# An attention stage ahead of an MLP: new slots for its steps, a new place for the rotary tables' load and for the spread of the softmax sums

## The chip, the cores and the metric

The kernel runs on one core of a Trainium2 chip. The metric is the device time of one execution in microseconds (us); lower is better. Engines are named as in the profile: PE (TensorE, matmul; PEld its weight loads), DVE (VectorE), ACT (ScalarE), POOL (GpSimd) and SP (SyncE, which here only issues DMA transfers). Each engine works off its own list of instructions in order; they meet through semaphores.

## What is computed

One layer of a hybrid encoder on 2048 tokens of width 1024, in float32:

```python
h = rms_norm(x, norm_mix_g)
qa, ka, va, qi, ki, wi, qb, kb, vb, zb, bb, ab = split(h @ w_in)
qa, ka, qi, ki = rope(...)                      # rotary: x1*cos - x2*sin, x2*cos + x1*sin
o_a = sparse_indexer_attention(...)             # 8 heads, 2 kv heads, width 64
      # index scores choose 256 keys per query; softmax attention over these,
      # keys admitted up to the end of the query's chunk of 64
o_b = gated_deltanet(...)                       # 4 heads, width 128, chunkwise delta rule
x = x + concat(o_a, o_b) @ w_out
h = rms_norm(x, norm_ffn_g)
x = x + square(relu(h @ w_ff1)) @ w_ff2         # 1024 -> 4096 -> 1024
out = rms_norm(x, norm_final_g)
```

The kernel computes the sparse attention as dense attention over all admitted keys with a bias that is hugely negative where a key was not chosen.

## The kernel before

Three stages follow one another: norm and input projection, the DeltaNet with index scores and the first part of the selection, and `attention_and_mlp`, which begins at 1526 us and runs to the end. The change lies in the third alone.

**Units.** Attention is cut into 16 tiles of 128 queries; a tile has four units of two heads, u = 4t + q, 64 in all. The steps of a unit are: `scores` on PE (q high and q low against the keys, in pieces of 512 keys; lines 2102 and 2103), `mask` on DVE (adds the bias, keeps the maximum; 1937, 1944), `exp` on ACT (1834), `rinv` on DVE (reciprocal of the sums; 1964), then in turns of two blocks of 128 keys (one turn in tiles 0 and 1, two in tiles 2 and 3) `transpose` on PE (2117), `high` on ACT (1823), `lower` on DVE (1957) and `product` on PE (2131, first with the high half of the probabilities, then with the low half). `spread` on PE (2139) copies the reciprocals along the 64 rows of the output by a matmul with the identity; `low` on ACT (1829) fetches the second half of the product, `finish` on DVE (1920 adds, 1923 multiplies by the spread) and `store` on SP (1651) end the unit. The product accumulates in one PSUM bank, O_BANK, columns 0 to 255. Transposes, values and the spread share a ring of two banks; whoever takes a ring bank waits until the one two places before has been read.

**Preparation.** Per tile there are three items, item 3t (keys) and 3t+1, 3t+2 (queries of the two kv groups): `prep_in` on SP (six transfers, lines 479 to 481), `cos` on DVE (1970), `sin` and `add` on POOL (1710, 1717), `round` on ACT (1846) and `prep_low` (1979 on DVE for keys, 1723 on POOL for queries), which raises `p_done`. The cosine and sine tables of a tile (`table_in`, line 1608) are in one buffer. `values` (2108) transposes the tile's values, `values_hi` and `values_low` split them, `values_out` (1617) stores them to memory and `values_back` (1626) loads them for each turn. Scores of units 4t and 4t+1 wait for items 3t and 3t+1, those of 4t+2 and 4t+3 for item 3t+2 also.

**MLP.** Tokens go through it in four blocks of 512. Each of its 288 weight units is loaded (`weights`, 1594), copied to a high half by ACT (`split`, 1807), its low half made by POOL (1695), and used by three matmuls a piece (2037 to 2039). The mixed rows come by `mix_in` (1668) in two buffers, with a copy on ACT (1800) and a subtraction on DVE (1912); `mix_in(0,4)` waits for all stores of units 0 to 15. While the MLP runs, ACT also searches the selection threshold of the late tiles (`probe`, 1750).

**The order.** `OverlapPlan` puts every step of every engine in a numbered slot; within a slot the steps of an engine follow `ORDER`. A slot has no duration and no barrier: it only fixes each engine's order. Units 0 to 15 (tiles 0 to 3) stand in the slots below 0, three slots apart (`begins(u)` = 3u - 58), the first dense matmul in slot 0; later units lie among the 147 slots of an MLP block, about 8.4 apart. The first slot is -71 before, -72 after. Where the steps of a unit stand is set by `attention`, the weights and splits by `mlp`, the ring by `number`.

Slots before of the start, as the plan gives them: SP -71 weights 0 and 1, values_in 0, prep_in 0 to 4, table_in 0; POOL -70 split 0 and 1, sin 0, add 0; -64 sin 1, add 1; PE -61 scores 0. SP at the end: -14 prep_in 14; -11 prep_in 15, table_in 5; -9 store 15, mix_in 0.

## Time and profile before

| | us |
|---|---|
| median of 3 runs | 3991.24 |
| lowest and highest | 3988.57 and 3998.67 |
| profiled execution, its own time | 3992.01 |
| its span (first to last instruction) | 3990.2 |
| PE busy | 3455.4 (87%) |
| ACT busy | 2182.6 (55%) |
| DVE busy | 2082.6 (52%) |
| POOL busy | 1373.3 (34%) |

The span cut into 40 equal slices of 99.8 us; a digit is the busy share in tenths, PEclk the TensorE clock granted, in tenths of full speed. The third stage begins in the 16th slice.

```profile
PE   6799847888888994578999879999888999988997
PEld 5688736777777773457777658787667878867886
DVE  5233036777777753445455465656457575433222
ACT  3212137666745543376966858696776944333232
POOL 3201043424254432223434323433323333334442
PEclk8899979999999996799999989999999999999999
```

### The profile page before, as it was taken

To read this page: it belongs to the slowest core of one execution; us is meant where nothing else is said; L and a number is where in the kernel's file an instruction comes from. 1 tells how busy PE (TensorE), PEld (TensorE's weight loads), DVE (VectorE), ACT (ScalarE), POOL (GpSimd) and SP (SyncE) were. 2 spreads that over 40 slices of the span, in tenths; PEclk is the share of its full clock that TensorE was granted. 3 is DMA by queue.
4 is the path that set the end of the run, shared out by engine and by line. 5 is a ranking of instruction groups with operands and counts; after the bars stand their busy time and mean duration, and the time that the engine had idled before them with its cause. 6 is when DMAs were issued, how large, how long until landed. Compare 5 with 4: busy or idle time off the path is not lost.

```text
span 3990.2 us, 47621 instructions
## 1 busy us (share of the span) xinstructions
PE 3455.4 (87%) x16994; PEld 2821.0 (71%) x16994; DVE 2082.6 (52%) x3582; ACT 2182.6 (55%) x3722; POOL 1373.3 (34%) x721
## 2 busy tenths in 40 slices
PE   6799847888888994578999879999888999988997
PEld 5688736777777773457777658787667878867886
DVE  5233036777777753445455465656457575433222
ACT  3212137666745543376966858696776944333232
POOL 3201043424254432223434323433323333334442
PEclk8899979999999996799999989999999999999999
DMA  3612162313332333323333333333333333342222
GB/s 106 248 63 79 64 171 60 111 50 76 100 81 79 85 124 106 101 86 96 107 109 115 97 118 105 124 106 113 111 118 108 109 101 105 100 132 80 97 97 71
DMA packets 326091, 409.63 MB, mean 103 GB/s; under 512 B 26065, under 2 KB 241233, under 8 KB 321489
## 3 DMA queue, kind: packets, MB, share of 16 engines
q1 hardware_dynamic: 320528, 370.94, 30.7%
q10 hardware_dynamic: 5328, 35.65, 2.3%
q8 instruction: 137, 2.24, 0.2%
q14 instruction: 98, 0.79, 0.1%
HBM read 331.62 MB, written 74.87 MB: 102 GB/s over the span
## 4 chain that ended last, share of the span: by engine, by line
PE 29%; ACT 16%; DVE 7%; issue 5%; POOL 2%; SPq 1%; DMA 1%; ACTq 0%; DVEq 0%; POOLq 0%
PE m_ps L2037 8%; PE m_ps L2039 8%; PE m_ps L2038 8%; ACT m_junk L1750 7%; ACT m_wh L1807 2%; PE m_ps L2131 2%; PE m_ps L2117 2%; ACT m_prob L1834 1%; ACT m_verdict L1752 1%; ACT m_trial L1756 1%; ACT m_phi L1823 1%; PE m_ps L2102 1%; PE m_ps L2080 1%; PE m_ps L2103 1%; ACT m_rl L1766 1%
## 5 line engine op out<-in xcount | busy, mean ns | idle before, releaser
L1695 POOL TENSOR_TENSOR m_wl<-m_raw,m_wh 128x1024 fp32r<-128x1024 f32 x288 | 715.2, 2484 | 1414.7 <-ACT m_wh L1807 1414.7
L2037 PE MATMUL m_ps<-m_ah,m_wh 128*128 128x512 f32 x1280 | 536.6, 419 | 71.4 <-DVE m_al L1896 42.2
L2039 PE MATMUL m_ps<-m_ah,m_wl 128*128 128x512 f32 x1280 | 512.5, 400 | 0.0
L2038 PE MATMUL m_ps<-m_al,m_wh 128*128 128x512 f32 x1280 | 511.2, 399 | 0.0
L2037 PE MATMUL m_ps<-m_th,m_wh 128*128 128x512 f32 x1024 | 428.7, 419 | 41.5 <-DVE m_tl L1876 25.1
L2039 PE MATMUL m_ps<-m_th,m_wl 128*128 128x512 f32 x1024 | 407.5, 398 | 0.0
L2038 PE MATMUL m_ps<-m_tl,m_wh 128*128 128x512 f32 x1024 | 406.3, 397 | 0.0
L1750 ACT ACTIVATE m_junk<-m_sc,m_trial 128x1152 int8<-128x1152 f32 (+7 forms) x248 | 401.6, 1619 | 1.3
L1807 ACT ACTIVATE m_wh<-m_raw 128x1024 fp32r<-128x1024 f32 x288 | 302.7, 1051 | 126.7 <-PE m_ps L2039 122.3
L2037 PEld LDWEIGHTS m_ps<-m_ah,m_wh 128*128 128x128 f32 x1280 | 247.4, 193 | 137.9 <-DVE m_al L1896 31.3
L1874 DVE TENSOR_TENSOR m_rl<-m_rl 128x512 f32<-128x512 f32 x128 | 93.8, 733 | 413.0 <-ACT m_th L1770 412.7
L1153 DVE SCALAR_TENSOR_TENSOR i_score<-i_relu,i_w,i_score 128x512 f32<-128x512 f32 (+3 forms) x266 | 272.3, 1031 | 50.3 <-ACT i_relu L1018 36.7
L1869 DVE TENSOR_TENSOR m_acc<-m_acc,m_ps 128x512 f32<-128x512 f32 x256 | 174.9, 684 | 231.6 <-PE m_ps L2039 230.0
L1823 ACT ACTIVATE m_phi<-m_ps 128x512 fp32r<-128x512 f32 (+1 forms) x288 | 163.9, 570 | 226.4 <-PE m_ps L2117 222.5
L2039 PEld LDWEIGHTS m_ps<-m_ah,m_wl 128*128 128x128 f32 x1280 | 247.2, 193 | 55.3
L2038 PEld LDWEIGHTS m_ps<-m_al,m_wh 128*128 128x128 f32 x1280 | 248.4, 194 | 47.6 <-issue 3.4
L1957 DVE TENSOR_TENSOR m_plo<-m_ps,m_phi 128x512 fp32r<-128x512 f32 (+1 forms) x288 | 189.2, 658 | 148.7 <-ACT m_phi L1823 147.3
L2037 PEld LDWEIGHTS m_ps<-m_th,m_wh 128*128 128x128 f32 x1024 | 196.7, 192 | 91.8 <-issue 34.4
L274 PE MATMUL ps<-xh,wh 128*128 128x512 f32 x576 | 226.9, 394 | 21.2 <-POOL wl L154 19.2
L1018 ACT ACTIVATE i_relu<-i_ps 128x512 f32<-128x512 f32 (+3 forms) x304 | 155.8, 544 | 148.8 <-PE i_ps L817 121.9
L2039 PEld LDWEIGHTS m_ps<-m_th,m_wl 128*128 128x128 f32 x1024 | 196.3, 192 | 43.7
L2038 PEld LDWEIGHTS m_ps<-m_tl,m_wh 128*128 128x128 f32 x1024 | 197.3, 193 | 41.6 <-issue 5.3
(306 smaller groups left out, 7559.9 us busy)
## 6 DMA issues: line engine op xcount, KB each, us to landing
m_raw<-w_units SPq DMA_DIRECT2D x288, 512.0 KB, 3.6
m_vals<-valsT SPq DMA_DIRECT2D x256, 128.0 KB, 3.7
p_raw<-w_proj SPq DMA_DIRECT2D x72, 256.0 KB, 3.9
projT<-work ACTq DMA_DIRECT2D x12, 1024.0 KB, 3.9
g_qkvz<-projT SPq DMA_DIRECT2D x16, 768.0 KB, 6.2
wraw<-w_proj SPq DMA_DIRECT2D x21, 512.0 KB, 3.5
projT<-p_out SPq DMA_DIRECT2D x36, 256.0 KB, 3.0
work<-xT SPq DMA_DIRECT2D x8, 1024.0 KB, 5.5
```

The lines of the kernel that those rows point to most:

```text
L274: nc.tensor.matmul(acc, wh[:, u, kc, :], xh[:, kc, tok], start=(kc == 0), stop=False)
L1018: nc.scalar.activation(relu[:, c % RELUS, 0:w], ips[:, c % 2, 0:w], ACT.Relu).then_inc(relu_done, 1)
L1153: nc.vector.scalar_tensor_tensor(out=to, in0=relu[:, c % RELUS, 0:w], scalar=w_idx[:, j, h:h + 1], in1=to, op0=ALU.mult, op1=ALU.add).then ...
L1695: nc.gpsimd.tensor_tensor(wl[:, n % 3, :], raw[:, n % 2, :], wh[:, n % 3, :].bitcast(fp32), ALU.subtract).then_inc(w_lo, 1)
L1750: turns.do(nc.scalar.activation(junk[:, 0:N], sc[:, 0:N], ACT.Sign, scale=-1.0, bias=trial[:, :].bitcast(fp32), accum_out=balance[:, :]))
L1807: nc.scalar.activation(wh[:, n % 3, :], raw[:, n % 2, :], ACT.Copy).then_inc(w_hi, 1)
L1823: nc.scalar.activation(p_hi[:, m % 2, 0:w], t_bank(r)[:, 0:w], ACT.Copy).then_inc(hi_done, 1)
L1869: nc.vector.tensor_tensor(acc[:, k, :], acc[:, k, :], f_bank(c), ALU.add).then_inc(y_added, 1)
L1957: nc.vector.tensor_tensor(p_lo[:, m % 2, 0:w], t_bank(r)[:, 0:w], p_hi[:, m % 2, 0:w].bitcast(fp32), ALU.subtract).then_inc(lo_done, 1)
L2037: nc.tensor.matmul(dst, hi, rh, start=first, stop=False)
L2038: nc.tensor.matmul(dst, hi, r_low, start=False, stop=False)
L2039: return nc.tensor.matmul(dst, lo, rh, start=False, stop=last)
```

## The change

It has four parts. (1) The first tables are loaded ahead of the rotated rows, and weights 0 to 3 after them; `table_in(t)` waits for the sine and cosine of the last item that uses the tables instead of for its low half. (2) The steps of a preparation item stand one slot or more apart, the first query item of a tile a unit sooner. (3) For units 0 to 15 (`alone`) mask, exp, high, lower, low, finish, store and the values' steps each move a slot or two later. (4) The spread goes to columns 256 to 511 of O_BANK and is put ahead of the first product of its unit, for all 64 units; it waits for `finish` of the unit before, and leaves the ring.

```diff
-        "sp": "weights store values_in values_out values_back prep_in table_in ...
+        "sp": "weights store values_in values_out values_back table_in prep_in ...
-        "pe": "product spread scores values transpose dense squares".split(),
+        "pe": "spread product scores values transpose dense squares".split(),
...
-        self.first = self.begins(-4) - 1
+        self.first = self.begins(-4) - 2
...
-            a = self.begins(4 * t + {"k": -4, 0: -2, 1: -1}[what])
-            prep_slot[i], prep_done[i] = a, a + 1
             before = i - 5 if i < 12 else 9 if i == 12 else i - 1
-            self.put("sp", self.first if before < 0 else prep_done[before] + 1, "prep_in", i, before)
+            load = self.first + (i > 0) if before < 0 else prep_done[before] + 1
+            a = max(self.begins(4 * t + {"k": -4, 0: -3, 1: -1}[what]), load + 2)
+            prep_at[i], prep_done[i] = a, a + 3
+            self.put("sp", load, "prep_in", i, before)
             self.put("dve", a, "cos", i)
-            for k in ("sin", "add"):
-                self.put("pool", a, k, i)
-            self.put("act", a + 1, "round", i)
-            self.put("dve" if what == "k" else "pool", a + 1, "prep_low", i)
+            self.put("pool", a, "sin", i)
+            self.put("pool", a + 1, "add", i)
+            self.put("act", a + 2, "round", i)
+            self.put("dve" if what == "k" else "pool", a + 3, "prep_low", i)
...
-            self.put("sp", self.first if t < 1 else prep_done[3 * t - 1] + 1, "table_in", t)
-            self.put("sp", self.first if t < 1 else self.begins(4 * t - 6) + 1, "values_in", t)
+            self.put("sp", self.first if t < 1 else prep_at[3 * t - 1] + 1, "table_in", t)
+            self.put("sp", self.first + 1 if t < 1 else self.begins(4 * t - 6) + 1, "values_in", t)
             a = self.begins(4 * t - 2)
-            kept[t] = a + 1
-            self.put("sp", a + 1, "values_out", t)
+            alone = 4 * t - 2 < 16
+            kept[t] = a + 1 + 2 * alone
+            self.put("sp", kept[t], "values_out", t)
             self.put("pe", a, "values", t)
-            self.put("act", a, "values_hi", t)
-            self.put("dve", a, "values_low", t)
+            self.put("act", a + alone, "values_hi", t)
+            self.put("dve", a + 2 * alone, "values_low", t)
...
+            alone = u < 16
...
                 self.put("pe", s, "scores", u, h, p)
-                self.put("dve", s, "mask", u, h, p)
-                mask_slot[u, h, p] = s
+                mask_slot[u, h, p] = s + alone
+                self.put("dve", s + alone, "mask", u, h, p)
                 if p == self.pieces(t) - 1:
-                    self.put("act", s + 1, "exp", u, h)
+                    self.put("act", s + 1 + alone, "exp", u, h)
...
                 self.put("pe", c + gap * i, "transpose", u, i)
-                self.put("act", c + gap * i, "high", u, i)
-                self.put("dve", c + gap * i, "lower", u, i)
-                end = c + gap * i + 2
+                self.put("act", c + gap * i + alone, "high", u, i)
+                self.put("dve", c + gap * i + 2 * alone, "lower", u, i)
+                end = c + gap * i + 2 + alone
+                if i == 0:
+                    self.put("pe", end, "spread", u)
                 self.put("pe", end, "product", u, i)
...
-            self.put("pe", end, "spread", u)
-            self.put("act", end, "low", u)
-            self.put("dve", end, "finish", u)
-            self.put("sp", end + 1, "store", u)
+            self.put("act", end + alone, "low", u)
+            self.put("dve", end + 2 * alone, "finish", u)
+            self.put("sp", end + 1 + 2 * alone, "store", u)
...
-            self.put("sp", self.first if n < 2 else self.first + 2 if n < 4 else self.unit_slot[n - 4] + 1, "weights", n)
-            s = self.unit_slot[n - 2] if n >= 2 else self.first + 1
+            self.put("sp", self.first + 2 if n < 2 else self.first + 3 if n < 4 else self.unit_slot[n - 4] + 1, "weights", n)
+            s = self.unit_slot[n - 2] if n >= 2 else self.first + 5
...
-        self.ring = [x for x in pe if x[0] in ("transpose", "spread", "values")]
+        self.ring = [x for x in pe if x[0] in ("transpose", "values")]
...
+        spread_bank = ps[0:HD, O_BANK, 2 * P:4 * P]
...
             def table_load(t):
                 if t:
-                    sp.wait_ge(p_done, 3 * t)
+                    sp.wait_ge(p_sin, 3 * t)
+                    sp.wait_ge(p_cos, 3 * t)
...
             def finish(u):
...
-                dve.wait_ge(ring_done, r + 1)
-                nc.vector.tensor_tensor(o, o, t_bank(r)[0:HD, 0:2 * P], ALU.mult).then_inc(norm_done, 1)
+                nc.vector.tensor_tensor(o, o, spread_bank, ALU.mult).then_inc(norm_done, 1)
...
             def invert(u):
                 dve.wait_ge(exp_done, 2 * u + 2)
                 if u >= 2:
-                    dve.wait_ge(ring_done, plan.ring_at["spread", u - 2] + 1)
+                    dve.wait_ge(pv_done, plan.turn[u - 2, 0] + 1)
...
             def product(u, i):
...
-                if i == 0 and u:
-                    pe.wait_ge(sum_done, u)
...
             def spread(u):
-                bank = ring_bank(plan.ring_at["spread", u])
+                if u:
+                    pe.wait_ge(norm_done, u)
                 pe.wait_ge(rinv_done, u + 1)
                 for h in range(2):
-                    last = nc.tensor.matmul(bank[0:HD, h * P:(h + 1) * P], rinv[:, u % 2, h:h + 1].to_broadcast([P, HD]),
-                                            ident[:, :], start=True, stop=True)
-                last.then_inc(ring_done, 1)
+                    nc.tensor.matmul(spread_bank[:, h * P:(h + 1) * P], rinv[:, u % 2, h:h + 1].to_broadcast([P, HD]),
+                                     ident[:, :], start=True, stop=True)
```

## Rows read from the trace of the kernel before

**Rows 1.** Stretches: from:to us, length, busy us (instructions) per engine, clock, DMA share, GB/s.
```profile
core 0: us, PE busy (x) PEld busy (x) DVE busy (x) ACT busy (x) POOL busy (x), PEclk, DMA share, GB/s
1526.00:1696.00 170.00, 76.80 (x308) 55.84 (x308) 66.27 (x207) 53.66 (x135) 52.17 (x49) 0.63 0.39 111
1526.00:1583.00 57.00, 12.79 (x42) 8.77 (x42) 12.23 (x45) 12.17 (x32) 19.85 (x22) 0.50 0.45 132
...
1850.00:3400.00 1550.00, 1434.14 (x6903) 1165.11 (x6902) 916.06 (x1644) 1107.73 (x1793) 555.59 (x264) 0.96 0.36 110
```

**Rows 2.** Timeline of the start: start us, us, engine line, what [idle before <- releaser].
```profile
1527.27 0.91 SPq L1594 DMA_DIRECT2D m_raw<-w_units  x2
...
1528.69 0.58 SPq L479 DMA_DIRECT2D m_acc<-projT  x1
...
1530.85 1.06 ACT L1807 ACTIVATE m_wh<-m_raw 128x1024 fp32r<-128x1024 f32 x1 [3.33 <-DMA m_raw<-w_units]
...
1531.98 4.64 POOL L1695 TENSOR_TENSOR m_wl<-m_raw,m_wh 128x1024 fp32r<-128x1024 f32 x2 [5.43 <-ACT m_wh L1807]
...
1546.08 0.43 SPq L1608 DMA_DIRECT2D m_table<-cosT  x1
1546.55 0.43 SPq L1608 DMA_DIRECT2D m_table<-sinT  x1
...
1548.68 0.42 DVE L1970 TENSOR_TENSOR m_acc<-m_acc,m_table 128x256 f32<-128x256 f32 x1 [26.16 <-DMA m_table<-sinT]
...
1555.06 1.26 POOL L1723 TENSOR_TENSOR m_qlo<-m_acc,m_qhi 128x512 fp32r<-128x512 f32 x1 [0.74 <-ACT m_qhi L1846]
...
1556.37 0.48 PE L2102 MATMUL m_ps<-m_keys,m_qhi 128*128 128x128 f32 x1 [23.06 <-POOL m_qlo L1723]
```

**Rows 3.** Timeline of tiles 0 and 1: table issue, product(1,0), scores(4).
```profile
1566.91 0.43 SPq L1608 DMA_DIRECT2D m_table<-cosT  x1
...
1573.37 0.58 PE L2131 MATMUL m_ps<-m_phi,m_vals 128*128 128x256 f32 x1 [8.58 <-DVE m_att L1920]
...
1583.39 0.58 PE L2102 MATMUL m_ps<-m_keys,m_qhi 128*128 128x256 f32 x1 [2.44 <-POOL m_qlo L1723]
```

**Rows 4.** Waits of PE, 1596 to 1675 us: us in total, times, longest.
```profile
PE m_ps L2102 <- POOL m_qlo L1723: 6.8, 3, 3.0
PE m_ps L2131 <- DVE m_att L1920: 4.8, 1, 4.8
PE m_ps L2131 <- DMA m_vals<-valsT: 3.8, 1, 3.8
```

**Rows 5.** Timeline: scores of units 5 and 6, and a product of unit 15.
```profile
1587.57 0.58 PE L2102 MATMUL m_ps<-m_keys,m_qhi 128*128 128x256 f32 x1
...
1593.09 0.58 PE L2102 MATMUL m_ps<-m_keys,m_qhi 128*128 128x256 f32 x1
...
1673.60 0.79 PE L2131 MATMUL m_ps<-m_plo,m_vals 128*128 128x256 f32 x2 [2.51 <-DVE m_plo L1957]
```

**Rows 6.** Timeline of the tail: last scores wait, mix loads, PE's restart.
```profile
1666.77 0.50 PE L2102 MATMUL m_ps<-m_keys,m_qhi 128*128 128x512 f32 x1 [1.73 <-POOL m_qlo L1723]
...
1683.81 15.97 SPq L1668 DMA_DIRECT2D m_tmp<-mixT  x8
...
1695.21 1.09 PE L2117 MATMUL m_ps<-m_ident,m_prob 128*128 128x128 f32 x4 [15.88 <-ACT m_prob L1834]
```

**Rows 7.** Waits of ACT, 1700 to 3990 us: us in total, times, longest.
```profile
ACT m_qhi L1846 <- POOL m_rot L1717: 38.8, 12, 8.7
...
ACT m_keys L1846 <- POOL m_rot L1717: 14.9, 7, 4.5
```

**Rows 8.** Chain that ended last: start us, us, what (first and last of 17).
```profile
1816.58 1.30 POOL m_rot L1717
...
2814.57 1.30 POOL m_rot L1717
```

**Rows 9.** Lines 2139 and 1923: xcount, ns min/median/max, first and last start us.
```profile
L2139 PE MATMUL m_ps<-m_ident,m_rinv x256: 272/273/477, 1562.2 to 3487.1; 128*64 128x128 f32 x128
...
L1923 DVE TENSOR_TENSOR m_att<-m_att,m_ps x64: 411/412/415, 1573.3 to 3487.8; 64x256 f32<-64x256 f32 x64
```

More of the change, by code:

```diff
@@ L1312 @@
     ORDER = {
-        "sp": "weights store values_in values_out values_back prep_in table_in bias_in score_in x_in mix_in out bias_out".split(),
+        "sp": "weights store values_in values_out values_back table_in prep_in bias_in score_in x_in mix_in out bias_out".split(),
         "pool": "split bias_set sin add prep_low".split(),
@@ L1375, in attention @@
     def attention(self):
-        prep_done, prep_slot, mask_slot, kept, product_slot = {}, {}, {}, {}, []
+        prep_at, prep_done, mask_slot, kept, product_slot = {}, {}, {}, {}, []
         for i, (t, what) in enumerate(self.prep_items):
-            a = self.begins(4 * t + {"k": -4, 0: -2, 1: -1}[what])
-            prep_slot[i], prep_done[i] = a, a + 1
             before = i - 5 if i < 12 else 9 if i == 12 else i - 1
-            self.put("sp", self.first if before < 0 else prep_done[before] + 1, "prep_in", i, before)
+            load = self.first + (i > 0) if before < 0 else prep_done[before] + 1
+            a = max(self.begins(4 * t + {"k": -4, 0: -3, 1: -1}[what]), load + 2)
+            prep_at[i], prep_done[i] = a, a + 3
+            self.put("sp", load, "prep_in", i, before)
@@ L1915, in finish @@
             def finish(u):
-                o, r = att[:, u % 2].rearrange("p a b -> p (a b)"), plan.ring_at["spread", u]
+                o = att[:, u % 2].rearrange("p a b -> p (a b)")
                 if u >= 2:
@@ L2087, in ring_bank @@
                         pe.wait_ge(lo_done, plan.turn[tuple(x)] + 1)
-                    elif what == "spread":
-                        pe.wait_ge(norm_done, x[0] + 1)
                     else:
```

## The prediction

> **What bounds the kernel now.** I read the stretches first, then the waits of the first attention units in order of time, then the waits of the MLP part. In the stretches [rows 1] the reader is to see that from 1526 us (third stage starts) to 1696 us (first output-projection matmul) TensorE is busy for 77 of 170 us at a mean granted clock of 0.63 (0.50, that is 1.2 GHz, for the first 57 us), while from 1850 to 3400 us it is busy for over 90% at 0.96. No engine is full in these 170 us: DVE adds up to 66, ACT to 54, POOL to 52. So the chain of steps is what counts there, and it has four parts.
> The head: SP issues two weights, the values and five rotated loads before the two tables. A rotated load is six transfers, and five loads take 17.4 us of issue (1528.69 to 1546.08), 3.47 each. So the tables go out at 1546.08 and 1546.55, the first multiply by cosine starts at 1548.68 and the first scores at 1556.37 [rows 2].
> Tile 1: its table is issued at 1566.91 behind rotated loads; the multiply, add and round of its keys stand behind it, and on ACT low(0) behind that round, and product(1,0) on PE waits 8.58 us [rows 3]. scores(4) starts at 1583.39 after waiting 2.44 us for POOL's low half of the queries.
> Tiles 2 to 4: PE waits 6.8 us in three waits for low halves of queries, 4.8 for DVE's finish (itself behind a table), 3.8 for a values transfer [rows 4] and 2.51 for a lower that stands behind a cosine [rows 5]: 17.9 us together. A unit that meets no such wait takes about 5.5 us (scores at 1587.57 and 1593.09) [rows 5].
> The tail: item 13 is done when PE's scores start at 1666.77, but SP then has two rotated loads (14, and 15 behind the end of 14), a table, values and a store to issue before the first mix load at 1683.81. The mix loads go in pairs, each with a copy and a subtraction, and PE starts again at 1695.21 after 15.88 us of idle [rows 6].
> In the MLP part PE's clock is 0.96 and its waits are short. ACT idles 38.8 us before 12 roundings of queries and 14.9 us before 7 of keys, all for POOL's add [rows 7]; 17 pieces of POOL and DVE on the rotated rows stand in the chain that ended last between 1816 and 2816 us, 21.9 us together; the group shows the first and the last [rows 8].
>
> **The change, part by part.** The profiled execution took 3992.01 us (span 3990.2, 1.8 around it); the median of the three runs is 3991.24, 0.8 less. The sum is made against 3992.
>
> Head. SP now issues tables (0.95), rotated load 0 (3.47), values, rotated loads 1 to 4 (13.9), and then weights. From 1527.27 the tables go out until 1528.2, load 0 until 1531.7; 2.1 us later (the sine table of tile 0 took 2.13 from issue to multiply [rows 2]) the first sine and cosine start, at 1533.8 instead of 1548.7. That is 15 us ahead, and I let none of it reach the scores: POOL's slot of item 1 holds split(0) and split(1) ahead of its sine. Weights are now issued at 1546.1 and 1546.6 behind 24 transfers; ACT's split came 3.58 us after the issue [rows 2], so 1549.7; its two copies take 1.06 each, POOL's first subtraction starts at 1550.8 and two take 4.64, to 1555.4. Then sine (1.26), add (1.26), round and the low half with its 0.74 before it (2.0): 1560.0. First scores 3.7 us later than now: +3.7.
>
> Tile 1. SP: weights 2 and 3 wait for the two splits (1555.4), rotated load 5 follows, load 6 waits for item 1 (1560.0) and is issued until 1563.4, values_out(0) lands 2 us later, four values_back (1.74), then the table, out by 1568.6 and landed at 1570.3: 0.8 later than now. Two steps now stand behind it: cos(3) precedes mask(1) and lower(0) on DVE, sin(3) precedes prep_low(2) on POOL, so scores(2) comes at 1572.5 instead of 1563.2. But items 4 and 5 are then off the path: cosine before mask, add and round a slot apart, and the 2.44 us wait of scores(4) goes. Two units of 5.3 us follow: scores(4) at 1583, as now. Head and tile 1 together: 0 (bounds -8, if the splits' transfers land before load 1 is used up, to +6, if load 7, which waits for prep_low(2), delays item 7).
>
> Tiles 1 to 4. Of the 17.9 us of waits [rows 4, 5]: the low-half waits (6.8) go, since sine, add, round, low have slots of their own and the cosine stands ahead of the masks; the 2.51 goes, cos(14) now stands behind lower(15,1); the values wait (3.79) stays in half, the eight x loads being issued next to it as before. The table's 4.80 becomes about 2: table(2) waits for sine and cosine of item 5, not for its low half, and by the queue's order I have it out at 1588, some 5 us ahead of now. That takes away 14. Against it: the spread needs its bank back, so PE waits for finish's second step, 0.41 us more than for its first, and mask(u+1) now comes ahead of finish(u-1) on DVE. The spread's four passes (0.27 us each at the full clock, 0.48 at the most [rows 9]) only move ahead of the product. Twelve units by 0.41 are 4.9; I charge 6. Sum -8. Following the slots gives the same: 1583 + 4 units of 5.5 + 2 for the table is scores(8) at 1607; eight units of 5.8 + 0.5 and 2 for the values make scores(16) 1659, for 1666.8 now [rows 6]. Bounds: -17.9 (nothing comes in place) and +7 (every wait stays and each unit pays 0.41 and a collision).
> The row shows 0.41 us for the step that reads the spread [rows 9]. The Trainium skill (PSUM — Partial Sum Buffer, Terms and rules) says that TensorE's writes and VectorE's reads of one bank and quadrant must be kept apart by semaphores whatever the columns. By it the spread's new place beside the product makes the next product wait for the normalisation as well; over all 64 units that would be 26 us if nothing hid it, and in the MLP part, where units are 30 us apart, the trace has nothing that waits so long. It bears out the charge and is no other result.
>
> Tail. mix_in(0,0) stands behind table_in(5), which now waits for sine and cosine of item 14 and no longer for its low half; rotated load 15 moves behind mix_in(0,2), store(15) too. From p_done of item 13 the way to the first mix load is 3.47 (load 14) + 2.4 (landing, estimated from the table's 2.13) + 1.3 (sine) + 0.95 (tables) + 0.9 (values) = 9 us, now 17 (1666.8 to 1683.8) [rows 6]. That is -8; load 15 between the third and fourth mix load gives 3.5 back. Sum -4.5 (bounds -11 to +3.5).
>
> MLP part. Items of later tiles get a slot (about 3.5 us) between cosine, add, round and low: ACT's 53.7 us of idle before the rounding mostly go, but PE only gains what was on its path. From below that is 0, from above 21.9 [rows 8]; I take -5, near the lower end, since probes, weight copies and relus queue on ACT anyway and take the place. The bound above zero: queries of the first half are now rounded a unit sooner and may have to wait for scores(4t-3); if each of 12 did so for as long as the mean of today's wait for POOL (3.2 us [rows 7]) and a fifth of it reached the end, that is +8.
>
> Sum: 0 - 8 - 4.5 - 5 = -17.5 on 3992: 3975.
>
> **The rivals.**
> A, slower: the table becomes the gate of each tile. prep_low(3t+2) on POOL stands behind sin(3t+3), mask(4t+1) and lower behind cos(3t+3), and the table is issued behind values_out, its 2 us landing and values_back. If at tiles 2, 3 and 4 this costs 8.6 us as at tile 1 (now about 6 in all), 20 us are added, the 8 of those tiles go and the head's 3.7 is not won back: 20 + 3.7 - 4.5 - 5 = +14, 4006. It decides as soon as the table lands over 5 us behind the last mask of the tile before. For it: SP carries some 17 us of issue per tile against 25 to 30 us. Against: now the table costs less with each tile (8.6, then 4.8 [rows 3, 4], then no wait of PE named by it) with SP as full.
> B, nothing moves: the waits on prep are replaced by PE's wait for finish, tail and MLP give only 4: 3988. For it: DVE and PE have the most work in the stretch (66 and 77 us [rows 1]) and pass it to each other twice a unit. Against: the largest of PE's waits there has POOL as its releaser, not DVE [rows 4].
> C, more: waits for prep go whole (-14 instead of -8), the tail gives 8, ACT's freed time reaches PE (-15): 3992 - 37 = 3955. The clock helps it: the stretch runs at 0.63 [rows 1], and if fewer gaps raise it, each matmul nears 0.27 from 0.48 us [rows 9].
>
> **How the numbers follow.** Forecast 0.50, A 0.13, B 0.22, C 0.15. The forecast's own range is 3963 to 3985. Over all cases 3951 to 4001 leaves out the far half of A and the end of C. What a measurement can tell from no change is 0.3%, 12 us: below 3979 or above 4003. Faster: 0.40 of the forecast and C: 0.55. Same: the other 0.10 and B: 0.32. Slower: A, 0.13.
>
> **What would show it.** Head: first cosine near 1534, and 20 us later the first split of POOL, first scores near 1560. If scores start before 1556 the splits weren't the gate. Tile 1: scores(4) near 1583, DVE idle before cos(3) until 1570. Tiles: no wait of scores for POOL's low half, PE's waits before the spread for DVE's finish of 0.5 to 1.5 us each. Tail: first dense matmul at 1683 (a gap of some 13 us to 1696 is the first three terms). MLP: ACT's idle before the rounding under 20 us, and the time from the first dense matmul to the end 5 us under its present 2294. Wrong would be a table wait at tiles 2 to 4 above 5 us (A), or the first dense matmul past 1692 (B).

## The result and the profile after

The changed kernel takes 3951.68 us (median of 4 runs, 3948.2 to 3953.18) against 3989.9 (4 runs, 3986.85 to 3998.67) on the same chip: 0.990 of the time, 95% interval 0.9888 to 0.9912. I had forecast 3975, so 38 us went where 17.5 were announced. The profiled executions are 39.3 us apart (3992.01 and 3952.70). A few executions of the kernels below ran in a second, slower state (one of 5547.6 us, at a granted clock of 0.58 where the others have 0.94); they count in no figure here.

The first view is the two stretches that answer to [rows 1]: the third stage up to its first output-projection matmul, and the MLP part.

```profile
core 0: us, PE busy (x) PEld busy (x) DVE busy (x) ACT busy (x) POOL busy (x), PEclk, DMA share, GB/s
1522.00:1678.00 156.00, 66.33 (x308) 52.59 (x309) 67.54 (x208) 53.56 (x136) 53.49 (x49) 0.65 0.43 121
...
1850.00:3400.00 1550.00, 1440.45 (x6992) 1169.15 (x6991) 912.47 (x1660) 1116.33 (x1800) 560.25 (x262) 0.97 0.36 110
```

To compare executions I read six times from each timeline, from the stage's first instruction on (a memset on POOL): the first scores of units 0, 4, 8 and 16, the first matmul of the output projection ("dense"), and from there to the end of the span.

| kernel | unit 0 | unit 4 | unit 8 | unit 16 | dense | dense to end |
|---|---|---|---|---|---|---|
| before | 30.4 | 57.5 | 85.8 | 140.8 | 170.0 | 2294.2 |
| changed | 34.4 | 56.9 | 78.2 | 129.8 | 155.0 | 2273.4 |
| changed again | 34.6 | 57.0 | 77.7 | 130.6 | 156.6 | 2272.8 |

So 15.0 us are gained ahead of the dense matmuls, 20.9 behind them, and 3.4 more because this execution's third stage began sooner (1522.53 for 1525.94 us); over all profiled executions here, whose first two stages are the same, that start varies from 1517.5 to 1528.0. The same rows cut at these two times split the later part, the last row being the kernel before's:

```profile
1677.55:3950.90 2273.35, 2092.17 (x9823) 1689.08 (x9821) 1171.26 (x2049) 1408.36 (x2249) 828.90 (x374) 0.96 0.34 105
```
```profile
1695.95:3990.20 2294.25, 2105.44 (x9823) 1701.79 (x9821) 1179.82 (x2049) 1407.80 (x2250) 823.16 (x374) 0.96 0.34 104
```

The same 9823 matmuls take 13.3 us less, and PE's idle time falls from 188.8 to 181.2.

The start, which answers to [rows 2, 3], in a timeline (start us, us, engine, line, what, idle before and its releaser):

```profile
1523.86 0.43 SPq L1614 DMA_DIRECT2D m_table<-cosT  x1
...
1529.79 0.99 DVE L1975 TENSOR_TENSOR m_acc<-m_acc,m_table 128x256 f32<-128x256 f32 x1 [10.66 <-DMA m_acc<-projT]
...
1542.67 10.04 SPq L1599 DMA_DIRECT2D m_raw<-w_units  x4
...
1547.70 4.64 POOL L1701 TENSOR_TENSOR m_wl<-m_raw,m_wh 128x1024 fp32r<-128x1024 f32 x2 [16.05 <-ACT m_wh L1813]
...
1552.30 1.27 POOL L1716 TENSOR_TENSOR m_acc<-m_acc,m_table 128x512 f32<-128x512 f32 x1
...
1556.96 0.47 PE L2105 MATMUL m_ps<-m_keys,m_qhi 128*128 128x128 f32 x1 [26.11 <-POOL m_qlo L1729]
...
1564.28 0.36 SPq L1614 DMA_DIRECT2D m_table<-cosT  x1
```

The first cosine runs 7.3 us after the stage's start instead of 22.7. Then POOL stands idle for 16.05 us before the first weight's subtraction, which its list puts ahead of the sine of item 1. The scores come 4.0 us later than before.

PE's waits from 1522 to 1677 us, in place of [rows 4] (columns as there):

```profile
PE m_ps L2141 <- DVE m_att L1928: 29.5, 15, 6.6
PE m_ps L2105 <- POOL m_qlo L1729: 27.1, 2, 26.1
...
PE m_ps L2120 <- ACT m_prob L1840: 13.1, 1, 13.1
...
PE m_ps L2132 <- DMA m_vals<-valsT: 2.9, 1, 2.9
```

Of the waits for low halves of queries only the first of the kernel is left (26.1) and one of 1.0 us, the last item's. In their place stand fifteen waits of the spread (line 2141) for DVE's finish, 29.5 us together and 0.6 to 6.6 us each, where I had expected 0.5 to 1.5 each. The tail, against [rows 6]:

```profile
1652.35 0.79 PE L2105 MATMUL m_ps<-m_keys,m_qhi 128*128 128x512 f32 x1 [1.01 <-POOL m_qlo L1729]
...
1661.84 0.42 SPq L1674 DMA_DIRECT2D m_tmp<-mixT  x1
...
1671.80 9.78 SPq L1674 DMA_DIRECT2D m_tmp<-mixT  x5
...
1676.81 1.09 PE L2120 MATMUL m_ps<-m_ident,m_prob 128*128 128x128 f32 x4 [13.12 <-ACT m_prob L1840]
```

The first mix load leaves 9.5 us after the last tile's scores, as computed (9), where it was 17.0; three of the eight leave before rotated load 15 and five behind it, from 1671.80 on.

And ACT's waits for POOL's add from 1700 us on, 53.7 us in [rows 7]:

```profile
ACT m_qhi L1852 <- POOL m_rot L1723: 6.2, 9, 2.7
```

### The profile page after: what moved, and what is told of

Same layout as the page of the kernel before. It is cut to its first block, busy times and chain, and to the rows that moved or that the text cites. A ratio compares the mean times of both kernels' runs of the same rounds, so it can differ in the third digit from the quotient of the medians.

```text
span 3950.9 us, 47570 instructions
## 1 busy us (share of the span) xinstructions
PE 3424.2 (87%) x16994; PEld 2799.0 (71%) x16994; DVE 2075.0 (53%) x3582; ACT 2183.2 (55%) x3722; POOL 1383.3 (35%) x721
## 4 chain that ended last, share of the span: by engine, by line
PE 30%; ACT 14%; DVE 8%; issue 5%; POOL 2%; DMA 1%; SPq 1%; ACTq 0%; DVEq 0%; POOLq 0%
PE m_ps L2042 8%; PE m_ps L2044 8%; PE m_ps L2043 8%; ACT m_junk L1756 6%; ACT m_wh L1813 2%; PE m_ps L2132 2%; PE m_ps L2120 2%; ACT m_prob L1840 1%; POOL m_wl L1701 1%; ACT m_verdict L1758 1%; ACT m_trial L1762 1%; PE m_ps L2105 1%; PE m_ps L2106 1%; PE m_ps L2085 1%; ACT m_phi L1829 1%
## 5 line engine op out<-in xcount | busy, mean ns | idle before, releaser
L2042 PE MATMUL m_ps<-m_th,m_wh 128*128 128x512 f32 x1024 | 426.7, 417 | 43.1 <-DVE m_tl L1882 22.7
L1962 DVE TENSOR_TENSOR m_plo<-m_ps,m_phi 128x512 fp32r<-128x512 f32 (+1 forms) x288 | 188.8, 656 | 135.5 <-ACT m_phi L1829 134.3
L1942 DVE CUSTOM_DVE_ANT_0 m_prob<-m_ps,m_bias 128x512 f32<-128x512 f32 (+3 forms) x320 | 191.6, 604 | 87.9 <-PE m_ps L2106 83.5
```

The lines of the kernel that those rows point to most:

```text
L1942: nc.vector.tensor_tensor_reduce(out=prob[:, u % 2, h, 512 * p:512 * p + w], in0=s_bank(n)[:, 0:w], in1=bias[:, 512 * p:512 * p + w], scal ...
L1962: nc.vector.tensor_tensor(p_lo[:, m % 2, 0:w], t_bank(r)[:, 0:w], p_hi[:, m % 2, 0:w].bitcast(fp32), ALU.subtract).then_inc(lo_done, 1)
L2042: nc.tensor.matmul(dst, hi, rh, start=first, stop=False)
```

## The experiments

Each kernel is one part of the change put into the kernel before, or the changed kernel with one thing altered. Ratios are to the kernel before on the same chip, with 95% intervals. Such a ratio is good to about 0.3% when two chips are compared: the kernel with early and late preparation stands at 0.9873 on one and 0.9903 on another. The stage times are gathered in one table behind the experiments; they come from one profiled execution each, and two executions of the same kernel differ by 1.6 us (changed) and 3.1 us (tables first) in the start of the dense matmuls.

**The later preparation alone.** Items of tiles 4 and up get the new slots, their query item starts a unit sooner, and the tables of tiles 5 and up wait for sine and cosine only; all else is as before.

```diff
+            old = t < 4
+            a = max(self.begins(4 * t + {"k": -4, 0: -3, 1: -1}[what]), load + 2)
+            if old:
+                a = self.begins(4 * t + {"k": -4, 0: -2, 1: -1}[what])
...
+            self.put("pool", a if old else a + 1, "add", i)
+            self.put("act", a + (1 if old else 2), "round", i)
+            self.put("dve" if what == "k" else "pool", a + (1 if old else 3), "prep_low", i)
```

> The kernel before with one part of the change: preparation items of tiles 4 to 15 get their new slots (cosine and sine in slot a, add a+1, round a+2, low half a+3, first query item a unit sooner); all else as before. Theory 1 (the MLP part gained 18 us because ACT no longer stands before a rounding for POOL's add: 53.7 us of that idle became 6.2): ACT's wait for POOL's add from 1700 us on falls below 15 us, first dense matmul stays within 3 us of 1696, and the time is 15 to 20 us shorter, 3970 to 3975. Theory 2 (the spread's new place gave it): ACT's waits fall as well but the time stays within 5 us of before, 3985 to 3995.

3963.05, 0.9939 (0.9924 to 0.9954): -24 us, a little more than the 15 to 20 expected; 21.5 lie behind the first dense matmul. So this part alone gives what the changed kernel gains there (20.9), four times my term. In its trace the idle before the rounding is 8.2 us:

```profile
ACT m_qhi L1856 <- POOL m_rot L1727: 8.2, 10, 3.2
```

PE's idle time behind the first dense matmul is 172.3 us, 16.5 less than before, its busy time 5.1 less. The chain that ended last still has 17 pieces of POOL and DVE on the rotated rows in it, 20.4 us together (before: 17 and 21.9). So here the gain did not come out of these pieces.

**The later rounding alone.** ACT's rounding and the low half behind it move two slots later, for tiles 5 and up; cosine, sine and add stay. The later loads and tables on SP, which the plan puts behind the low half, move with it.

```diff
-            self.put("act", a + 1, "round", i)
-            self.put("dve" if what == "k" else "pool", a + 1, "prep_low", i)
+            self.put("act", a + (1 if t < 5 else 3), "round", i)
+            self.put("dve" if what == "k" else "pool", a + (1 if t < 5 else 3), "prep_low", i)
```

> The kernel before, with ACT's rounding and the low half behind it two slots later for items of tiles 5 to 15, and nothing else: cosine, sine and add stay in slot a, the first query item is not sooner. Theory 1 (the loss was ACT's: it stood before the rounding for POOL's add while its own relus and weight copies waited behind it): nearly all of late_only's 24 us, 3963 to 3970, and ACT's wait for POOL's add from 1700 us below 15 us. Rival (POOL's sine and add in one slot are the loss: POOL waits there for DVE's cosine and its weight subtraction comes late): at most a third of it, 3980 to 3988, though ACT's wait falls as well.

3970.61, 0.9944 (0.9928 to 0.996): -22. Behind the first dense matmul the gain is 16.7 us for the 21.5 of the late preparation, and the next kernel, which spaces all the steps, is 9.6 us faster on the same chip. So moving the rounding gives two thirds to three quarters of it. What it leaves is POOL's own wait for DVE's cosine, 28.7 us in this part as before, which the late preparation lowers to 7.5; whether the rest of the gain comes from that was not tested. ACT then waits once for POOL's add:

```profile
ACT m_qhi L1853 <- POOL m_rot L1724: 0.4, 1, 0.4
```

**The later preparation without the unit's lead.** As the first kernel, with -2 in place of -3.

> late_only without its other half: items of tiles 4 to 15 are spaced (sine a, add a+1, round a+2, low half a+3), but the first query item of a tile keeps its place two units ahead instead of three. Theory 1 (the spacing is what counts): within 4 us of late_only, 3961 to 3968. Rival (the unit sooner counts, since now two items of a tile stand a unit apart and share one buffer): half of the gain is lost, 3972 to 3980.

3961.0, 0.9926 (0.9911 to 0.994), 2 us under the late preparation, on another chip: the query item's earlier start isn't needed. In the trace, too, the two are close (dense matmuls 1.3 us sooner, the part behind them 4.6 us longer).

**The rounding sooner.** The wait is made larger: for tiles 5 and up the rounding stands in the add's own slot, a slot ahead of where it was.

```diff
-            self.put("act", a + 1, "round", i)
+            self.put("act", a + (1 if t < 5 else 0), "round", i)
```

> The kernel before with ACT's rounding one slot sooner for items of tiles 5 to 15, in the slot of the cosine (low half as before): ACT stands before it from the cosine's slot on. Theory (ACT's idle before the rounding reaches the end at about 0.4 us per us, 21 us for 50 us): its idle there grows from 54 us to 90 to 130 us and the time by 15 to 30 us, 4005 to 4020. Rival (only what was on the path already counts, further idle of ACT is hidden by the work queued ahead of PE): within 6 us of before.

4061.49, 1.0193 (1.0176 to 1.021): 77 us slower where I had expected 15 to 30. ACT now waits 143.9 us:

```profile
ACT m_qhi L1853 <- POOL m_rot L1724: 99.0, 22, 8.7
...
ACT m_keys L1853 <- POOL m_rot L1724: 44.9, 11, 6.6
```

That is 90 us more than before, and the part behind the first dense matmul takes 72.3 us more, 0.8 per us of ACT's idle. Taking the 53.7 us away gave 0.3 (16.7 of 53.3, the later rounding) to 0.5 (21.5 of 45.5, the later preparation). The direction of the theory held, the size missed by more than twofold. Where it reaches PE can be read from PE's waits for the high half (line 1823 of before), which ACT's list puts behind the rounding, from the first dense matmul on, first in the kernel before and then here:

```profile
PE m_ps L2131 <- ACT m_phi L1823: 6.5, 6, 1.8
```
```profile
PE m_ps L2138 <- ACT m_phi L1830: 34.1, 15, 8.0
```

**The early preparation alone.** Items of tiles 0 to 3 get the new slots, and their tables wait for sine and cosine only.

```diff
-                if t:
+                if t and t > 4:
                     sp.wait_ge(p_done, 3 * t)
+                elif t:
+                    sp.wait_ge(p_sin, 3 * t)
+                    sp.wait_ge(p_cos, 3 * t)
```

> The kernel before with one part of the change: preparation items of tiles 0 to 3 get their new slots and the tables of tiles 1 to 4 wait for sine and cosine; loads of the start, steps of the units and spread as before. Theory 1 (the waits of scores for POOL's low half and for the table are what the first 16 units lost): scores(8) some 5 us sooner, first dense matmul 8 to 12 us sooner (it also takes item 15's load out of the way of the first mix load), time 3978 to 3983. Rival (the steps of the units must move as well, else the cosine only blocks another step): first dense matmul within 3 us of 1696 and time within 4 us of before.

3973.79, 0.9962 (0.9947 to 0.9977): -15. The dense matmuls start 15.7 us sooner, where I had expected 8 to 12; half of it is there by unit 4 (-7.9), most of it by unit 8 (-13.7), and the way from unit 16 to dense is 28.1 us for 29.2. Tables leave 20.2, 36.5, 56.5 and 77.2 us after the stage's start, before 20.1, 41.0, 67.6 and 93.7. PE's waits for low halves, from the stage's start to dense, before and then here:

```profile
PE m_ps L2102 <- POOL m_qlo L1723: 32.3, 5, 23.1
```
```profile
PE m_ps L2112 <- POOL m_qlo L1733: 30.3, 4, 22.3
```

They hardly fall. What went are the two waits of a unit's first product for DVE's finish, 8.58 and 4.80 us [rows 3, 4], both of which I had put down to the tables.

**The head alone.** Tables first, one more slot of lead, weights 0 to 3 and the splits behind the rotated loads.

```diff
-            self.put("sp", self.first if n < 2 else self.first + 2 if n < 4 else ...
-            s = self.unit_slot[n - 2] if n >= 2 else self.first + 1
+            self.put("sp", self.first + 2 if n < 2 else self.first + 3 if n < 4 else ...
+            s = self.unit_slot[n - 2] if n >= 2 else self.first + 5
```

> The kernel before with one part of the change: first tables loaded ahead of the rotated rows, weights 0 to 3 after them, their splits five slots later. Theory 1 (POOL's two splits gate item 1): first cosine 15 us sooner but first scores 3 to 5 us later, and no gain at the first dense matmul: 3988 to 3996. Rival (the head start is worth something once items of tile 0 are done early): first scores before 1556 and time 5 to 15 us shorter.

3984.51, 0.9998 (0.9987 to 1.001). The first scores come at 34.7 instead of 30.4 us and the dense matmuls at 166.6 for 170.0, a difference that the timed runs don't bear out.

**The spread alone.** Its place in O_BANK, its wait for the finish before, no ring.

```diff
-        self.ring = [x for x in pe if x[0] in ("transpose", "spread", "values")]
+        self.ring = [x for x in pe if x[0] in ("transpose", "values")]
```

> The kernel before with one part of the change: the spread in columns 256 to 511 of the product's bank, ahead of the first product of its unit, waiting for finish of the unit before, and out of the ring. Theory 1: nothing to gain in the MLP part (its trace had 3 us of waits on the ring), in the first 16 units the wait for finish costs 0.4 us a unit: 3990 to 3997. Theory 2 (the spread frees the ring and PE in the MLP part): 3970 to 3980, all of it after the first dense matmul.

3985.88, 0.9996 (0.9987 to 1.0006): nothing. Behind the dense matmul PE is busy for 9.2 us less and idle for 4.8 more; the attention ahead of it takes 3.6 us longer. What it wins in the one part it gives back in the other.

**Early and late preparation together.** The two kernels above in one.

> The kernel before with the new slots for the preparation items of all tiles and nothing else (start, units and spread as before). Theory (the change's gain is the sum of its two preparation parts, 15 and 24 us, and its three other parts give nothing): 3948 to 3956, the changed kernel's own time. Rival (the parts overlap, one wait freed twice): 3960 to 3968.

3942.6 (median of three), 0.9873 (0.9852 to 0.9894): -51. The stages are read from its second measurement:

> early_late again, beside the changed kernel. Theory (only the preparation's slots gain, the rest of the change costs 0 to 6 us through the later head): 3944 to 3952, at or a little below the changed kernel. Rival (the rest is worth something too): 4 us or more above the changed kernel.

3946.24, 0.9903 (0.9889 to 0.9918): -39, the sum of 15 and 24; the first measurement was more than that. Beside it on the same chip stood the changed kernel:

> The changed kernel itself, run beside the other two so that they are compared on one chip: ratio to before 0.988 to 0.991, as when it was first measured.

3949.88, 0.9911 (0.9896 to 0.9926). The intervals overlap: the kernel with the old head and the old spread is at least as fast, and the rest of the change costs 0 to 4 us.

**Another head: tables ahead of the rotated rows, weights 0 and 1 still first.** To early and late preparation one exchange in the order of SP is added; the splits stay where they were.

```diff
-        "sp": "weights store values_in values_out values_back prep_in table_in ...
+        "sp": "weights store values_in values_out values_back table_in prep_in ...
```

> The kernel before with the new slots for preparation items of all tiles (early_only and late_only together) and one change of the start: the tables go ahead of the rotated rows in the first slot, while weights 0 and 1 stay ahead of both and their splits stay where they were. Units and spread as before. Theory (the head start is eaten in the change by the two splits, which stand ahead of item 1 and wait for weights loaded last): splits are done by 1537, first scores 14 us sooner than now at 1542, the table of tile 1 goes out some 8 us sooner, and with the 39 us of the two parts the time is 3935 to 3943. Rival (the first tiles are bound by SP's queue, so scores(4) comes when it did): 3947 to 3955.

3940.85, 0.9876 (0.9859 to 0.9892). The first scores come at 17.9 us:

```profile
PE m_ps L2107 <- POOL m_qlo L1728: 18.6, 4, 10.4
...
PE m_ps L2136 <- DMA m_vals<-valsT: 10.9, 1, 10.9
```

The second line is why little of this lasts: the first product now waits 10.9 us for its values, 3.5 in the kernel with the old head.

The second measurement shares its chip with early_late_2 and changed_again:

> table_first again, beside the changed kernel and early_late. Theory (first scores 14 us sooner and the tables of the next tiles with them): 8 to 14 us below the changed kernel and 4 to 10 below early_late. Rival (SP's queue gives the head start back): within 3 us of early_late.

3941.66, 0.9892 (0.9877 to 0.9906): 8 us under the changed kernel, 4.6 under the one with the old head. Of the 12 us by which its first scores are sooner, 4 are left at unit 4 and 2 to 5 at dense.

**The changed kernel with its splits out of the way.** Weights 0 and 1 in slot first + 13, their splits in first + 22, weights 2 and 3 in first + 25.

```diff
-            self.put("sp", self.first + 2 if n < 2 else self.first + 3 if n < 4 else ...
-            s = self.unit_slot[n - 2] if n >= 2 else self.first + 5
+            self.put("sp", self.first + 13 if n < 2 else self.first + 25 if n < 4 else ...
+            s = self.unit_slot[n - 2] if n >= 2 else self.first + 22
```

> The changed kernel with weights 0 and 1 loaded in slot first + 13, their splits in first + 22 and weights 2 and 3 in first + 25, where POOL idles in tile 1. Theory (as for table_first: POOL's splits gate the head): first scores near 1540 instead of 1557, first dense matmul 6 to 10 us sooner, time 3941 to 3946. Rival (POOL and ACT have no room in tile 1 and the splits cost there what they cost at the head): within 4 us of the changed kernel's 3952.

3939.77, 0.987 (0.9854 to 0.9886): first scores at 17.0, dense at 143.7, 12 us under the changed kernel's first measurement (another chip). What held its first scores at 34.4 us were the two splits on POOL.

**The changed kernel with the start of the kernel before, tables first.**

> The changed kernel with the start of table_first: weights 0 and 1 ahead of the tables in the first slot, their splits a slot later, weights 2 and 3 two slots later; all else as changed. If table_first's 11 us over the changed kernel come from the start alone: 3936 to 3943. If they come from the old slots of the units and the old place of the spread: 3948 to 3954.

3942.68, 0.9873 (0.9854 to 0.9891), 9 us under the changed kernel's first measurement, dense at 144.3: much the same gain by the other way, leaving the weights first in SP's queue.

**Without the later unit slots.** `alone = 0` in the changed kernel.

> The changed kernel with the steps of units 0 to 15 back in their old slots (mask, exp, high, lower, low, finish, store and the values' steps); all else as changed. Theory (these shifts change who stands behind whom, but no wait of the 16 units that counts): within 5 us of the changed kernel's 3952. Rival (they are what takes the cosine and the low half out of the units' way): first dense matmul 8 to 15 us later and time 3960 to 3967.

3947.5 (median of four), 0.989 (0.9869 to 0.9911), dense at 153.5: the slots of units 0 to 15 did not need to move.

**The handshake of the spread.** In the changed kernel the spreads of units 0 to 15 alternate between banks 0 and 1, which the MLP uses only later; a spread waits for the finish two units back, the product for the first step of the finish before it.

```diff
-        spread_bank = ps[0:HD, O_BANK, 2 * P:4 * P]
+        spread_bank = lambda u: ps[0:HD, u % 2, 0:2 * P] if u < 16 else ps[0:HD, O_BANK, 2 * P:4 * P]
```

> The changed kernel with the spread of units 0 to 15 alternating between PSUM banks 0 and 1, which are free until the first dense matmul: the spread waits for finish of two units before, and the product for finish's first step alone. It measures the handshake that the prediction charged with 6 us (PE's waits before the spread for DVE's finish are 29.5 us in all in the changed kernel). Theory (DVE is behind in any case, since finish stands behind two masks; the handshake itself is 0.4 us): waits move from the spread to the product, gain 0 to 4 us. Rival (the whole 29.5 us are the handshake's): first dense matmul 10 us sooner or more, 3942 or less.

3946.89, 0.9881 (0.9864 to 0.9898). Dense comes at 149.7 us for 155.0 and 156.6, so this handshake cost 5 to 7 us, 3 to 4 of them between units 4 and 16, for which I had charged 6; I then expected 0 to 4 in all. Single executions differ by up to 3 us here, and the medians by 3 to 5, so only its rough size is shown. PE's wait for DVE's finish, now by the product, is 12.6 us shorter:

```profile
PE m_ps L2136 <- DVE m_att L1926: 16.9, 10, 5.9
```

| kernel | unit 0 | unit 4 | unit 8 | unit 16 | dense | dense to end |
|---|---|---|---|---|---|---|
| late preparation | 30.4 | 57.3 | 85.6 | 142.6 | 166.5 | 2272.7 |
| later rounding | 30.5 | 57.6 | 86.0 | 143.3 | 172.2 | 2277.5 |
| late, without lead | 30.5 | 57.5 | 85.9 | 141.4 | 165.2 | 2277.3 |
| rounding sooner | 30.5 | 57.4 | 85.7 | 140.7 | 169.5 | 2366.5 |
| early preparation | 29.6 | 49.6 | 72.1 | 126.2 | 154.3 | 2295.9 |
| head | 34.7 | 59.1 | 83.8 | 137.6 | 166.6 | 2293.1 |
| spread | 30.6 | 58.0 | 86.7 | 145.2 | 173.6 | 2289.8 |
| early and late | 29.5 | 49.6 | 71.3 | 124.8 | 148.9 | 2272.9 |
| tables first | 17.9 | 45.2 | 67.7 | 119.8 | 143.5 | 2272.2 |
| tables first, again | 18.0 | 45.4 | 67.9 | 122.5 | 146.6 | 2275.1 |
| splits later | 17.0 | 46.4 | 68.1 | 117.7 | 143.7 | 2271.6 |
| old start, tables first | 17.9 | 48.5 | 70.2 | 118.2 | 144.3 | 2273.9 |
| unit slots as before | 34.2 | 53.9 | 76.9 | 128.2 | 153.5 | 2271.4 |
| two banks | 34.5 | 55.2 | 77.5 | 125.0 | 149.7 | 2272.6 |

The last column falls into two groups with one outlier: whatever has the late preparation is between 2271 and 2278, whatever lacks it between 2289 and 2296, and the kernel with the rounding sooner is at 2366. The changes ahead of dense leave that column alone within some 3 us. The spread alone takes 4.4 off it and the late preparation 21.5, but the changed kernel, which has both, only 20.9.

## Why the prediction was wrong

**Head, +3.7: right.** First scores 4.0 us later; the subtractions, the sine and the low half ran in the order and at the lengths that I had laid out (POOL's pair 4.64 us, then 1.27 and 1.26). Splits later and tables first show that it was the splits on POOL, as said. What I did not see is that the change left 16 to 17 us of first scores, and some 9 to 12 us of time, lying in this spot.

**Tile 1, up to scores(4) 0: right in sum.** 57.5 became 56.9.

**Tiles 1 to 4, -8: the sum close, its parts only half borne out.** From unit 4 to unit 16 the changed kernel takes 72.9 us for 83.3, so -10.4. The handshake costs 3 to 4 us of that stretch by single traces, not 6 (two banks -3.1 to -3.8, the spread alone +3.9). With it, the waits removed come to the 14 that I had named; but the early preparation without the handshake gains only 6.7 us between these units, after 7.9 ahead of them, and in it 4.9 of the 6.8 us of low-half waits that I had struck out are still there. What its trace has lost are the waits that I had put down to the tables: the table of tile 2 leaves 4.7 us sooner in the changed kernel, as I had counted (5), and 11 in the early preparation. Rival A's gate (the table) did not close at all: in the changed kernel the second table leaves at 41.8 us, 0.8 later than before as computed, but the third at 62.9 for 67.6 and the fourth at 83.1 for 93.7.

**Tail, -4.5: right.** The first mix load leaves 9.5 us after the scores for 17.0, and from unit 16 to dense it is 25.2 us for 29.2, so -4.0. The gap before the restart is 13.12 for 15.88.

**MLP part, -5: wrong, and this is the step that failed.** It measured -20.9, and -21.5 with the late preparation alone. ACT's idle before the roundings fell as forecast (under 20 us, measured 6.2); mis-sized was what that is worth. I wrote that PE gains only what was on its path, and took a value near the lower end "since probes, weight copies and relus queue on ACT anyway and take the place". The later rounding refutes that sentence: with nothing moved to an earlier slot and the roundings' wait gone, the part is 16.7 us shorter, 12.2 of it PE's idle time (188.8 to 176.6 us). Rows of before show how such a wait reaches PE, and the 8.7 of [rows 7] pointed at them:

```profile
2162.07 1.05 ACT L1807 ACTIVATE m_wh<-m_raw 128x1024 fp32r<-128x1024 f32 x1
...
2167.47 3.20 DVE L2017 TENSOR_TENSOR_SCAN m_sc<-m_tie 128x1408 f32<-128x1408 bf16 x1
...
2167.80 3.96 POOL L1717 TENSOR_TENSOR m_rot<-m_rot 128x512 f32<-128x512 f32 x1
...
2171.79 0.63 ACT L1846 ACTIVATE m_qhi<-m_rot 128x512 fp32r<-128x512 f32 x1 [8.67 <-POOL m_rot L1717]
2172.33 0.58 ACT L1766 ACTIVATE m_rl<-m_ps 128x512 f32<-128x512 f32 x1
```

From 2163.12 to 2171.79 ACT does nothing, because the rounding at the head of its list waits for POOL. Behind it stand the relu of an MLP piece and its square, the high half of an attention turn and the next weight copy. PE's rows of the same microseconds show when they could have run: the last matmul of the relu's piece ended at 2167.51 and the turn's transposes at 2168.41, so the relu started 4.8 us late and the high half (2173.48) 5.1 us late. PE bore it until here:

```profile
2167.81 0.60 PE L2117 MATMUL m_ps<-m_ident,m_prob 128*128 128x128 f32 x4
...
2174.22 0.46 PE L2131 MATMUL m_ps<-m_phi,m_vals 128*128 128x256 f32 x2
2175.76 0.50 PE L2131 MATMUL m_ps<-m_plo,m_vals 128*128 128x256 f32 x2 [1.08 <-DVE m_plo L1957]
```

Its 1.08 us of idle are put down to DVE's lower, and nothing in the row names the rounding three engines back. That is how such a wait hides: 8.67 us on ACT became about 1 on PE, under another's name. The reader should look at what comes behind a wait on its own engine, not at the busy pieces that the chain lists.
The Trainium skill (TensorE: Matmul & The Clock Gate, Architectural detail: the array is 16× 32×32, not 1× 128×128, at "Engine queue depths") says that ACT's and DVE's queues are strictly first in, first out; that agrees with these rows, where a relu whose input had been finished for 4.8 us stood behind a rounding.

The upper bound of the term, 21.9 from the chain's pieces [rows 8], holds the measured value by chance. In the kernel with the late preparation these pieces are nearly all still there (20.4 us) though 21.5 us were gained. In the later rounding they do shrink, to 5.6 us, with a gain of 16.7; with the rounding sooner they grow to 61.1 us, some 39 more, and the end moves 72. So they are no bound, and no measure that holds from kernel to kernel. ACT's idle before the rounding does better only in direction: -45.5 us gives -21.5, -53.3 gives -16.7, +90.2 gives +72.3. A third to a half of the 53.7 us of [rows 7] would have made the term -18 to -27, but that share was read from these runs afterwards; nothing in the rows of before gave it.

**The rivals.** C (3955, at 0.15) came nearest in size and named the right mechanism with "ACT's freed time reaches PE (-15)"; its tail of -8 and its -14 for the waits didn't come (-4.0 and -10.4), and more came in the MLP part, so that its sum is as near as it is by luck. A and B fell, though what B named, PE's waits for DVE's finish in place of those on the preparation, is what the trace shows (29.5 us). The bound on the slow side of the MLP part, queries that wait because they are rounded a unit sooner, showed nowhere, and the kernel without that lead is as fast.

**What stays open.** The share of PE's busy time in the gain. Of the changed kernel's 20.9 us behind the first dense matmul, 13.3 are busy time and only 7.6 idle, while the late preparation alone has 5.1 and 16.5. With the spread in O_BANK the 9823 later matmuls are busy for 2090 to 2096 us, without it for 2097 to 2111 (2123 with the rounding sooner), though the spread alone made no kernel faster; whether those matmuls wait inside their recorded time or run faster was not separated. Nor was it shown why an added microsecond of ACT's idle costs 0.8 and a removed one brings only 0.3 to 0.5.

## What to carry to other kernels

Price a wait at the head of an engine's list by that engine's idle time in front of it and by what is queued behind it, not by how much of the releaser is in the critical chain; in this kernel, where the idle engine also feeds the busiest one, a third to a half of it came back as gain, and 0.8 of it was lost where the wait grew. The cheapest cure was to put the waiting instruction two slots later and leave its producers alone; it gave two thirds to three quarters of what spacing all the steps gave. When a load is moved to the front of a queue, look for what else the same engine is made to do first: here moving the tables gained nothing until the two splits stood clear of the first query item, and then 5 to 12 us.

## What the runs showed of the hardware

POOL's add of 128x512 takes 1.26 to 1.28 us by itself and 3.96 us beside DVE's scan in the fence above: the scan began 0.33 us ahead of it and ended at 2170.67, and the add ended 1.09 us after that, as if nearly all of it had run once the scan was done. It is not a single case: at 2365.93 us of the same trace an add takes 4.18 us and ends 1.06 us after a scan of 3.35, and in the changed kernel one of 3.67 us ends 1.08 after a scan of 2.81. The length is not only the profile's: ACT's rounding, which waits for the add, starts 0.03 us after its end. The Trainium skill (SBUF — State Buffer, SBUF: two separate sides) says that a DVE operation with two SBUF inputs and a GpSimd operation that reads SBUF hold a shared port pair in turn, the one that starts first for its whole length. These three rows agree with it (line 2017 gives the scan the same row of SBUF for both inputs); no run here moved the two apart to test it.

PE's busy time is no measure of this attention stretch. The changed kernel spends 65.9 us of 155.0 on its matmuls and the second measurement of tables first 78.0 of 146.6, at granted clocks of 0.65 and 0.62, and the second is the shorter.
